# The first gate product ahead of the sums of squares behind DeltaNet, and weights rounded by half panels

## What is computed

```python
for l in range(2):
    mx, mc = nine modulation vectors of c and of c_ctx      # silu(c) @ ada_w[l] + ada_b[l]
    h  = h + 0.5 * gate * swiglu(modulate(rms_norm(h)))      # first FFN, hidden width 2816
    u  = modulate(rms_norm(h))
    gm, qkv, z, ab, cq, ckv, gates = split(u @ w_in[l])
    ya = chunked gMLP(gm);  yc = latent attention(cq, ckv)
    o  = bidirectional gated DeltaNet(qkv, ab)               # 4 heads, forwards + backwards
    yb = rms_norm(o, per head) * silu(z)
    m  = sigmoid(ga)*(ya @ w_a) + sigmoid(gb)*(yb @ w_b) + sigmoid(gc)*(yc @ w_c)
    h  = h + gate * (m @ w_out)
    h  = h + 0.5 * gate * swiglu(modulate(rms_norm(h)))      # second FFN
```

## Time and profile before

| | us |
|---|---|
| median of 3 runs (lowest, highest) | 2563.38 (2560.06, 2568.40) |
| the profiled execution, its own time | 2561.39 |
| its span, first to last instruction | 2559.6 |
| TensorE busy with matmuls | 2450.7 (96% of the span) |
| VectorE, ScalarE, GpSimd busy | 1474.0, 940.6, 78.4 |
| mean granted clock of TensorE | 0.981 |

### The profile page before, as it was taken

The page is one execution under the profiler, slowest core; times in us unless marked ns, Lnnn a source line. Parts: engine busy times, 40 slices in busy tenths (PEclk is TensorE's granted clock), DMA queues, the critical chain, the costliest instruction groups (busy, mean ns, idle before and its releaser), DMA issues.

```text
span 2559.6 us, 37980 instructions
## 1 busy us (share of the span) xinstructions
PE 2450.7 (96%) x15918; PEld 2079.2 (81%) x15918; DVE 1474.0 (58%) x2299; ACT 940.6 (37%) x1523; POOL 78.4 (3%) x110
## 2 busy tenths in 40 slices
PE   5999999999989999999999999999999989999999
PEld 3888877857878888878888778888886778899999
DVE  5877656255657464677755453333354667566655
ACT  2322223355553322233222232222245554354543
POOL 0000000000023000000000000000000003100000
PEclk8999999989999899999999999999999999999999
DMA  7544542201200043325555432222231220044554
GB/s 273 209 181 182 183 155 107 83 34 40 93 34 3 18 164 115 132 98 195 185 186 192 148 111 97 99 99 99 99 116 66 83 83 2 3 180 166 179 183 165
DMA packets 44664, 309.67 MB, mean 121 GB/s; under 512 B 5072, under 2 KB 6224, under 8 KB 7632
## 3 DMA queue, kind: packets, MB, share of 16 engines
q1 hardware_dynamic: 44208, 305.98, 32.9%
q10 hardware_dynamic: 288, 1.27, 0.1%
HBM read 306.18 MB, written 1.05 MB: 120 GB/s over the span
## 4 chain that ended last, share of the span: by engine, by line
PE 88%; DVE 6%; ACT 2%; issue 2%; DMA 1%; POOL 0%; SPq 0%; ACTq 0%; DVEq 0%
PE bank L1414 73%; PE bank L1767 6%; PE bank L1407 2%; PE bank L1712 1%; PE bank L1691 1%; DVE u_lo L2058 1%; DVE sq L2050 1%; DVE w_lo L2011 1%; PE bank L1445 1%; PE bank L1627 1%; DVE work L2480 1%; DMA mod_par<-in_mod 0%; ACT w_hi L895 0%; PE bank L1700 0%; PE bank L1457 0%
## 5 line engine op out<-in xcount | busy, mean ns | idle before, releaser
L2011 DVE TENSOR_TENSOR w_lo<-ring,w_hi 128x1024 fp32r<-128x1024 f32 x420 | 511.0, 1224 | 727.1 <-ACT w_hi L895 722.3
L1414 PE MATMUL bank<-u_hi,w_hi 128*128 128x512 f32 (+1 forms) x2272 | 814.9, 359 | 31.1 <-DVE w_lo L2011 17.3
L1414 PE MATMUL bank<-u_hi,w_lo 128*128 128x512 f32 (+1 forms) x2272 | 806.7, 355 | 0.0
L1414 PE MATMUL bank<-u_lo,w_hi 128*128 128x512 f32 (+1 forms) x2272 | 806.5, 355 | 0.0
L895 ACT ACTIVATE w_hi<-ring 128x1024 fp32r<-128x1024 f32 x420 | 443.3, 1059 | 877.3 <-PE bank L1414 875.3
L1414 PEld LDWEIGHTS bank<-u_hi,w_hi 128*128 128x128 f32 x2272 | 433.4, 191 | 99.5 <-issue 21.6
L1414 PEld LDWEIGHTS bank<-u_lo,w_hi 128*128 128x128 f32 x2272 | 432.9, 191 | 59.5
L1414 PEld LDWEIGHTS bank<-u_hi,w_lo 128*128 128x128 f32 x2272 | 433.5, 191 | 58.3
L1414 PE MATMUL bank<-hidden_hi,w_hi 128*128 128x512 f32 (+1 forms) x722 | 260.6, 361 | 0.0
L1414 PE MATMUL bank<-hidden_hi,w_lo 128*128 128x512 f32 (+1 forms) x722 | 259.9, 360 | 0.0
L1414 PE MATMUL bank<-hidden_lo,w_hi 128*128 128x512 f32 (+1 forms) x722 | 259.9, 360 | 0.0
(11 more groups left out here) (231 smaller groups left out, 2465.4 us busy)
## 6 DMA issues: line engine op xcount, KB each, us to landing
ring<-in_wts SPq DMA_DIRECT2D x288, 1024.0 KB, 4.8
h<-in_x SPq DMA_DIRECT2D x8, 256.0 KB, 4.1
par<-in_par ACTq DMA_DIRECT2D x2, 620.0 KB, 6.1
out<-h SPq DMA_DIRECT2D x8, 128.0 KB, 3.5
cst<-in_cst SPq DMA_DIRECT2D x1, 704.0 KB, 11.9
mod_par<-in_mod SPq DMA_DIRECT2D x1, 96.0 KB, 12.2
cond<-in_c SPq DMA_DIRECT2D x1, 8.0 KB, 1.8
```

Of the source, the lines that this page charges most:

```text
L1414: last = weights.used(pe.matmul(out, lhs[a], rhs[b], start=start and n == 0, stop=stop and n == 2))
L2011: tt(w_lo[:, b % HALVES, :], half_source(n % RING, part), w_hi[:, b % HALVES, :].bitcast(F32), ALU.subtract).then_inc(panel_left[n % RING] ...
```

## The change

Three things, one of which is only there for another.

1. TensorE issues the product `("gate", 0, 0)` right behind `outs(1, 3)`, ahead of the waits for the outputs and of the sums of squares, and leaves it out of the loop further down.
2. So that this product's bank is free there, the banks of DeltaNet are named from the number of that product: its bank and the next are the `STATE` pair, the other two the `FRESH` pair. The numbers are 106 and 312, so that `STATE` is banks 2 and 3 in layer 0, and 0 and 1 in layer 1, where it was 1 and 3.
3. Weights are rounded by halves. `Splits` counts halves, and each `norm` takes one more: ScalarE behind the fourth item from the end (three more `u_hi` come behind it), VectorE behind the last `u_lo`. In the panels of `AHEAD`, the second ones of an FFN, ada products wait until the first half's rest is made, and stand ahead of the second half's.

```diff
-        FRESH, STATE = [bank[0], bank[2]], [bank[1], bank[3]]
+        FIRST_GATE = [number[l, "gate", 0, 0] % 4 for l in range(DEPTH)]
+        DELTA_BANKS = [([bank[(n + 2) % 4], bank[(n + 3) % 4]], [bank[n], bank[n + 1]]) for n in FIRST_GATE]
...
+        AHEAD = [SPLITS[split_before[START[key]] + 1] for key in START if key[1] == "gu"]
+
         class Splits:
...
+            def half(self):
+                panel, part = divmod(self.n, 2)
+                if panel < len(SPLITS):
+                    self.one(SPLITS[panel], panel, part)
+                    self.n += 1
+
+            def to(self, panels):
+                while self.n < 2 * min(panels, len(SPLITS)):
+                    self.half()
...
@@ ScalarE, norm
                 elif len(PARTS[l, i]) > 1 and n == 3:
                     root(1)
+                if n == len(items) - 4:
+                    splits.half()
...
@@ TensorE, behind DeltaNet
                 for d in range(2):
                     outs(d, 3)
+                std([(l, "gate", 0, 0)], w, u, None, 0)
...
-                            std([(l, "gate", 2 * gq + c, b)], w, u, None, 0)
+                            if gq or b or c:
+                                std([(l, "gate", 2 * gq + c, b)], w, u, None, 0)
...
@@ VectorE
-            def rest_of_panel(n, sb):
+            def rest_of_half(n, sb, part):
                 nonlocal next_ada
-                while next_ada < n:
+                while part == (n in AHEAD) and next_ada < n:
                     ada_products(next_ada)
                     next_ada = next(ada_panels)
...
```

More of the change, by code:

```diff
@@ L805, in __init__ @@
                 self.one, self.n = one, 0
+            def half(self):
[6 more added lines that the diff above has]
+                    self.half()
             def next(self, count=1):
[L808 to L811 removed]
+                self.to(self.n // 2 + count)
             def past(self, start, half):
                 end = split_before[START[start[0], "ukv"]] if start[1] == "low" else len(SPLITS)
[L816 to L817 removed]
+                self.to(min(split_before[START[start]] + half // 2 + 2, end))
             def upto(self, n):
[L821 to L822 removed]
+                self.to(split_before[min(n, N_PANELS)])
         @block.sync
@@ L919, in norm @@
                 act.wait_ge(mods_ready, UNITS * l + 3 * i + 2)
-                for n, (part, k) in enumerate(norm_items(l, i)):
+                items = norm_items(l, i)
+                for n, (part, k) in enumerate(items):
                     if l == i == 0 and n == 1:
@@ L1196, in _ @@
                 keep_values(3)
+                FRESH, STATE = DELTA_BANKS[l]
                 def scaled_heads(dst, src, factor):
```

39 lines of the change are left out of this document (15 added, 24 removed).

## The result

The changed kernel took 2552.02 us (median of 7 executions, 2547.51 to 2554.29) beside 2562.53 us for the kernel before (7 executions, 2560.06 to 2568.63). The ratio is 0.9938, 95% interval 0.9924 to 0.9951: faster, by 16 us as the ratio has it and by 10.5 us between the two medians. Forecast was a gain of 20.5 us between the medians, 19.1 us against the profiled execution of before. (The two medians alone stand at 0.9959, outside that interval.) One thing has to be known to read these numbers: executions of the kernel before lie in two groups, most of them at 2560.1 to 2563.4 us and 2567.3 to 2573.1 us (two at 2564, one at 2575.7), and the lower one holds five of the seven above and the profiled one (2561.4), but only 8 of 26 in the first series of the experiments, whose median is 2568.6.

What follows compares the result with a forecast made beforehand. TensorE, 88% of the chain, was taken as the bound, gaining only where idle or at low clock. Norms 9.5, idle 3.0 and clock 6.6 us summed to 19.1, from 2561.39 to a forecast of 2542 us, range 2534 to 2553.

Steps and rivals of the forecast that it cites:

- Norms: Six norms: the half of weights rounded ahead saves 6.1 us of waits and 3.4 of clock, together 9.5 us.
- the clock term: Behind layer 0's second FFN norm: with little idle left the clock doesn't fall, 3.4 us won, between 0 and 3.4.
- VectorE's backlog: FFN pairs with ada panels: VectorE keeps up with a margin of 0.2 us; if missed, under 1 us lost.
- Idle at DeltaNet's ends: TensorE's waits for the first squares, 1.59 us in layer 0 and 1.38 in layer 1, go: 3.0 us won.
- Clock behind DeltaNet: Around the sums of squares the clock falls later and for less time: 3.2 us won in layer 0, 3.4 in layer 1.
- low stretches fall differently from run to run, and I take 2542: Whole span: 2542.3 us from the profiled execution, the runs' median 2.0 above it, so 2542 taken as forecast.
- for a clock that falls elsewhere: Whole kernel: a chance of 0.04 kept for low stretches in other places, with no size given.
- (a): DeltaNet's ends: the low stretches only move, the sums lower the clock as long as before; 2548.9 us, chance 0.18.
- (b): DeltaNet's ends: no clock fall, since no idle time is left ahead of the sums; 2535.3 us, chance 0.12.
- (c): Norms: they give only the clock, as ScalarE's rounding and VectorE's ada products take back the rest; 2550.6 us, chance 0.07.
- (d): DeltaNet's ends: gate product not ready at its new place, only the norms' 9.5 us stay; 2551.9 us, chance 0.03.
- (e): Norms: slower than before, ScalarE's new rounding waits for the panel's load, 4.8 us in six norms; 2577 us, chance 0.04.

Runs made afterwards that it cites:

- e3: The kernel before with only the other banks for DeltaNet's state and outputs, instruction order unchanged: 2568.29 us against 2568.61, ratio 1.000.
- e7: The changed kernel with 14 matmuls on constants put in once, behind layer 0's mixing norm's product: 2552.77 us, ratio 0.9946.
- e8: The changed kernel with ScalarE's rounding of the half ahead behind the norm's last u_hi: 2551.45 us, ratio 0.9944.
- e2: The changed kernel with the first gate product back behind the sums and the old banks, so only the half ahead in norms: 2558.64 us, ratio 0.9965.
- e11: e10 with 12 and 10 more matmuls on constants meant for two waits at DeltaNet's start in each layer: 2542.92 us, ratio 0.9902.
- e5: The changed kernel with the sums of squares spread between the second gate product's matmuls, and the spreading matmuls one product later: 2540.04 us, ratio 0.9904.
- e1: The changed kernel without the half ahead in the norms, so only the gate product moved, with its banks: 2562.09 us, ratio 0.9969.
- e9: e5 with the sums of squares in a row again, behind the second gate product: 2553.36 us, ratio 0.9945.
- e6: The changed kernel with 14 matmuls on constants ahead of each norm's streamed product, where TensorE waits: 2548.31 us, ratio 0.9936.
- e10: e5 with 8 matmuls on constants ahead of each norm's streamed product: 2541.42 us, ratio 0.9896.

## Why the prediction came out as it did

**The sign and the range held, the gain was half as large against the profile shown.** 2552.0 lies in the range of 2534 to 2553, at its upper end; 2542 was 10 us too low. The change's own places did not fail:

- **Norms.** Behind a last `u_lo` the next product starts 1.67 us (435.06 - 433.39) where 2.28 - 0.6 = 1.68 was worked out, and a norm is 0.54 us longer (0.6). The first FFN gave 2.8 us for 2.3, layer 1's first FFN 1.0 for 1.0. In the second FFN 6.2 for 7.1, clock included. There the clock term was too large: the stretch of 6.8 us began at 1142.9, and TensorE idled until 1144.33, so that 5.4 us of it slowed work, which is 2.7 us and not 3.4 (an estimate from these rows; 2.5 came). VectorE's backlog held: no new wait for a rest in a pair with ada panels.
- **Idle at DeltaNet's ends.** 1.59 and 1.38 us went. The 0.3 us wait at the spreading in layer 1 went too; I had kept it.
- **Clock behind DeltaNet.** The fall was put 4.5 us into the sums, and stands 4.7 us into them; 10.6 us low were expected and 10.1 came, 3.4 and 3.4 in layer 1. The two ends are 5.1 and 5.4 us shorter than in the profile of before, forecast 4.8 each; against e3's profile they are 3.4 and 3.9 us shorter.

Added up over the first FFNs, DeltaNet's ends, the second FFN of layer 0 and three norms, the forecast is -18.2 us and the trace -18.9. Against e3's profile, where several low stretches of before stand otherwise, it is -17.1.

**The step that failed is the last sentence of the sum**, "low stretches fall differently from run to run, and I take 2542". It took the clock of all other stages from one profiled execution, at 0 change. They cost 9.6 us where -0.9 was forecast: mixing and DeltaNet of layer 0 +4.9, the norm ahead of layer 1's mixing +2.6, layer 1's mixing and DeltaNet +1.3, the last norm and FFN +1.4, the start -0.6. In windows of 1 us, the low stretches of the whole span add up to 99 us before and 106 after (109 in each of the second profiles), though 20.5 of them went at the three places of the forecast. The page says it in one number, the mean granted clock: 0.981 before, 0.979 after.

Two things were mixed in it. First, the profile of before was a favourable one: the second (e3) has the same stretch at 704 us, and a norm of 16.1. Measured against that profile the changed kernel is 16.9 us faster in its first profile and 17.3 in its second, and against the 26 executions of its series 16.9 between medians, so that 2 of the missing 10 us are left (2568.6 - 19.1 = 2549.5 for 2551.7). Second, low stretches come and go in stages that an edit doesn't touch, and between two executions of one order of instructions: before against e3 differ by 7.6 us of span in this way, e7 and e8 have them in two norms where both profiles of the changed kernel have none. Whether an edit, however small, changes where they fall, or each execution does it by itself, these runs don't separate. So it is partly luck of the base that the median comes out 10 us above the forecast and not 2. I had the words for it ("for a clock that falls elsewhere", 0.04) and should have given it the width of the two groups of times, 8 us. What stays open is which of the possible places are hit in a given execution. The runs show what such places have in common (rows of sums, waits with small matmuls), not how to foresee the hit from the trace of before.

**Why a low stretch costs less than half its length in some places.** The waits on TensorE change with it. The rest of weights ahead of DeltaNet in layer 1 was waited for 1.69 us before and 0.23 after, and I took that for a gain of the change (e2's expectation). It isn't: in the profiles from before to e11 the wait is 1.69 or 1.70 us where no low stretch stands just ahead (before, e5, e7, e8) and 0.2 to 0.3 in the nine where one does. TensorE comes later and finds the rest made. A norm pays 2.0 to 2.4 us for a stretch of 6.7, not 3.4, for the same reason.

**The rivals.** (a) falls as a statement on DeltaNet's end (e1) and is nearest to the truth as one on the whole span, for a reason that it didn't have. (b), no fall once the idle time is gone, falls: e9 and the changed kernel show the clock fall in sums without a gap. It was put beside the rule of the Trainium skill, TensorE: Matmul & The Clock Gate, section "Why this matters for your kernels", that idle gaps between bursts drop the clock. Where TensorE idles, e6 and e10 agree with it (fillers in the norm's wait keep the clock up); for the sums the measurement decides against it as the only cause. The same page says in its Part 1, "What's actually happening", that the gate isn't in step with the kernel's start, so that one kernel shows different slow matmuls from run to run; e3 against before is that, and its advice that this can be left out of an estimate did not hold for differences of 0.3%. (c) falls by the waits and by e8. (d) falls by the row at 858.74, (e) by the norms' lengths: none grew by more than 0.54 us at full clock.

**The checks promised.** The waits at 58.6 and 1144.3 are gone or 0.16, those forecast at 0.3 to 0.7 are 0.16, since a wait for `u_lo` of 0.32 us took the rest: the longer norm shows as the wait for its last items. That is the 0.8 us by which the waits for `u_lo` grew.

## What to carry to other kernels

Cut two traces at the same instructions and compare stage by stage before believing a sum: here nearly all of the forecast (17 to 19 us, by the profile that one compares with) was there, and 10 us of clock elsewhere hid it. Do the same for matmuls put into a wait: e11's were meant for one and stood behind it. Where single executions of one kernel lie in groups, look at a profile of each group before using one as the base, and give a change of under 1% at least their distance as width. A row of tiny matmuls costs more than its time: the same 32 and 16 sums, spread between large matmuls, gave 5.6 us at their own place (10.1 against e9, the same matmuls in a row), and the kernel with them (e5, 2540.0 us) is faster than both kernels of this study.

## What was unexpected of the hardware

- The clock fell in a stretch in which TensorE had no gap: in a row of sums with one moving column, 0.22 us each, 4.7 us after their start, in e9 after 2.7 (layer 0) and 2.8 us (layer 1). The same sums, four behind every three matmuls of 512 columns, left it at 1.00 for 19.5 us.
- Where low stretches fall is not fixed by the order of instructions. Two profiles of the changed kernel agree to the microsecond at 701, 1872, 1954, 1971, 2077, 2094 and 2210 us, but two of the kernel before differ in at least two places (704.9 and 1513.9 us stand in one only), and e8, with its second FFN's norm within 0.7 us of where the changed kernel has it, has one there that neither of that kernel's profiles has.
- A higher mean clock is no shorter time: e11 had 0.989 and 2542.9 us, e5 0.987 and 2540.0; the matmuls that e11 adds raise the one and lengthen the other.
- A matmul on 128x128 constants in f32 takes 0.22 us (14 in 3.1 us), twice what I had read off rows of other 128x128 matmuls.
